# An encoder layer on one core: the mixer's projection units in quarters over all levels, VectorE's unit work one level later, ScalarE's high parts behind its keys, and transposes of the out projection moved up

## What is computed

```python
def hybrid_mixer(u, w_in, attn_sink, attn_out_norm, lb_fwd, lb_bwd, hg_out_norm, w_out, layer):
    proj = u @ w_in                       # (512, 1024) @ (1024, 3328)
    q, k, v, hq, hf_fwd, hf_bwd, hi, hg = jnp.split(proj, cuts, axis=-1)
    q = partial_rope(q...); k = partial_rope(k...)
    att = rmsnorm(windowed_gqa_sink(q, k, v, attn_sink), attn_out_norm)   # 8 heads, window 128
    qh = sigmoid(hq); vh = silu(hi)                                       # 4 heads of 128
    o_fwd = hgrn2_direction(qh, vh, hf_fwd, lbf)      # gated linear recurrence, f = lb + (1-lb)*sigmoid
    o_bwd = flip(hgrn2_direction(flip(qh), flip(vh), flip(hf_bwd), lbb))
    o = rmsnorm(o_fwd + o_bwd, hg_out_norm) * silu(hg)
    return concatenate([att, o]) @ w_out
```

## Time and profile before

| | |
|---|---|
| median of 3 runs | 1089.02 us (1088.95 to 1090.69) |
| the profiled execution, own time | 1084.51 us |
| its span, first to last instruction | 1082.7 us |
| TensorE busy | 1055.2 us, 97% |
| VectorE, ScalarE, GpSimd busy | 39%, 34%, 42% |
| mean granted TensorE clock | 0.990 of full |

### The profile page before, as it was taken

How to read it: one execution, slowest core, us unless ns; L and a number is a source line. 1 busy time by engine, 2 the same in 40 slices (tenths; PEclk the granted TensorE clock), 3 DMA queues, 4 the chain that set the end, 5 groups by cost and what they waited for, 6 DMA issues and landing times.

```text
span 1082.7 us, 13358 instructions
## 1 busy us (share of the span) xinstructions
PE 1055.2 (97%) x5075; PEld 872.4 (81%) x5075; DVE 423.3 (39%) x605; ACT 371.3 (34%) x558; POOL 452.8 (42%) x299
## 2 busy tenths in 40 slices
PE   6999999999999999999998989999999999999997
PEld 5988888888888878888776768788888888888886
DVE  5443434343000351556554565545343434320103
ACT  6322222222122354416665465343222222221211
POOL 3444444444444158842524123035444444444440
PEclk9999999999999999999998989999999999999999
DMA  6333333333433244331111013024333333333312
GB/s 217 97 98 96 98 96 97 97 97 98 136 98 97 59 134 117 78 97 40 39 37 43 1 41 116 20 78 117 92 101 89 103 88 101 91 102 114 97 51 78
DMA packets 136300, 96.00 MB, mean 89 GB/s; under 512 B 11442, under 2 KB 120387, under 8 KB 136260
## 3 DMA queue, kind: packets, MB, share of 16 engines
q1 hardware_dynamic: 136080, 95.43, 29.3%
q10 hardware_dynamic: 180, 0.02, 0.0%
HBM read 93.34 MB, written 2.10 MB: 88 GB/s over the span
## 4 chain that ended last, share of the span: by engine, by line
PE 93%; DVE 3%; ACT 2%; issue 1%; DMA 1%; ACTq 0%; DVEq 0%
PE ps L873 19%; PE ps L874 18%; PE ps L875 18%; PE ps L880 9%; PE ps L881 9%; PE ps L882 9%; PE ps L1039 2%; PE ps L1131 2%; PE ps L1154 2%; PE ps L1073 1%; DVE YB L1326 1%; PE ps L1141 1%; ACT SQX L540 1%; PE ps L898 1%; PE ps L1050 1%
## 5 line engine op out<-in xcount | busy, mean ns | idle before, releaser
L439 POOL TENSOR_TENSOR WL<-raw,WH 128x1024 fp32r<-128x1024 f32 x132 | 317.9, 2410 | 426.2 <-ACT WH L518 426.2
L873 PE MATMUL ps<-XH,WH 128*128 128x512 f32 (+1 forms) x944 | 359.6, 381 | 0.1
L875 PE MATMUL ps<-XH,WL 128*128 128x512 f32 (+1 forms) x944 | 355.0, 376 | 0.0
L874 PE MATMUL ps<-XL,WH 128*128 128x512 f32 (+1 forms) x944 | 354.9, 376 | 0.0
L518 ACT ACTIVATE WH<-raw 128x1024 fp32r<-128x1024 f32 x162 | 171.1, 1057 | 341.5 <-PE ps L875 187.3
L873 PEld LDWEIGHTS ps<-XH,WH 128*128 128x128 f32 x944 | 178.7, 189 | 41.0 <-issue 9.5
L875 PEld LDWEIGHTS ps<-XH,WL 128*128 128x128 f32 x944 | 178.4, 189 | 32.2
L874 PEld LDWEIGHTS ps<-XL,WH 128*128 128x128 f32 x944 | 178.6, 189 | 31.5 <-issue 0.5
L456 POOL TENSOR_TENSOR WL<-raw,WH 128x256 fp32r<-128x256 f32 x120 | 95.1, 825 | 127.8 <-ACT WH L518 127.6
L880 PE MATMUL ps<-WH,hh 128*128 128x512 f32 x352 | 137.1, 390 | 0.0
L882 PE MATMUL ps<-WL,hh 128*128 128x512 f32 x352 | 137.0, 389 | 0.0
(11 more groups left out here) (164 smaller groups left out, 896.7 us busy)
## 6 DMA issues: line engine op xcount, KB each, us to landing
raw<-ffn_w_gate SPq DMA_DIRECT2D x44, 512.0 KB, 3.7
raw<-ffn_w_up SPq DMA_DIRECT2D x44, 512.0 KB, 3.7
raw<-ffn_w_down SPq DMA_DIRECT2D x44, 512.0 KB, 3.7
raw<-w_in SPq DMA_DIRECT2D x22, 512.0 KB, 3.6
raw<-w_out SPq DMA_DIRECT2D x8, 512.0 KB, 3.2
X<-x SPq DMA_DIRECT2D x4, 512.0 KB, 7.0
raw<-w_in SPq DMA_DIRECT2D x8, 256.0 KB, 3.3
out<-X SPq DMA_DIRECT2D x8, 256.0 KB, 2.0
```

The costliest lines, as they stand in the source:

```text
L439: pool.tensor_tensor(low, raw[:, s, :], high.bitcast(fp32), ALU.subtract).then_inc(lo_done, 1)
L873: nc.tensor.matmul(dst, WH[:, s, w], xh, start=first, stop=False)
L874: nc.tensor.matmul(dst, WH[:, s, w], xl, start=False, stop=False)
L875: return nc.tensor.matmul(dst, WL[:, s, w], xh, start=False, stop=last)
```

## The change

**Table.** `mixer_beats` gives each level a count of quarters (2 of the 8 blocks, 6 matmuls): 3 in levels 0 to 9, 2 in level 10, then 1 or 2 in every level to 40, but for 22 (none). Units 7 and 8 now come whole before the loop (before: 7 alone). `values` comes behind a level's parts, a transpose of a `k`, `v` or `q` unit two levels after the unit is done, ahead of the parts.

**VectorE.** `copy_even` and `take_attention` come earlier in a level; the sum of a block's weights is a function of its own, one level earlier; the copy or gate of a unit comes one level after the unit is done, and behind `att_max`. Root, scaling and transposes of the attention and of the recurrence outputs move one level down.

**ScalarE.** `copy_odd` is first in a level, the keys next, and a unit's high part (`ahead`) behind them. `high_o(0)` moves behind the loop.

**Output projection.** `turn_att(2)`, `turn_att(3)` and `turn(2, 0)` go up, the last from behind chunk 2's eight blocks into their middle; with them `high_att(3)`, `low_att(3)`, and `add_y(2, 3)` goes ahead of `split_low(2, 2)`. `turn_o(1)` goes behind the last `values`.

No matmul, elementwise operation or load is added or taken away.

```diff
-    counts = [(2, 1, 2, 1, 2, 1, 2, 1, 2, 1, 1), (0, 1, 1, 1, 1, 1, 1, 1, 0, 0, 0), (0, 1, 1, 1, 1, 1, 1, 1, 0, 0, 0),
-              (0, 1, 1, 1, 1, 1, 1, 0, 0, 0, 0)]
-    halves = [(n, p) for n in range(4 + 3, MIX_UNITS) for p in range(2)]
...
+    counts = (3,) * 10 + (2,) + (1, 1, 1, 1, 1, 2, 1, 1, 1, 1, 1) + (0, 2, 1, 2, 1, 1, 1, 1, 1, 1, 1) + (1, 2, 1, 2, 1, 2, 1, 2, 0, 0, 0)
+    parts = [(n, p) for n in range(4 + 3, MIX_UNITS) for p in range(4)]
+    return parts[:8], [[parts.pop(8) for _ in range(c)] for c in counts]
...
+        MADE = [[n for n, p in parts if p == 3] for parts in BEAT] + [[], []]
...
-        TURN_BEAT, HIGH_BEAT, ROOT_BEAT = 41, 42, 36
+        TURN_BEAT, HIGH_BEAT, ROOT_BEAT = 42, 43, 37
... ScalarE
-                ahead(MIX + min(at + 3, MIX_UNITS + 3))
+                if att_item(i - 2) and i % 2:
+                    copy_odd(i - 2)
                 if g < 7:
                     mix_keys(h, g)
                 elif g >= 8:
                     copy_scores(h, g)
-                if att_item(i - 2) and i % 2:
-                    copy_odd(i - 2)
+                ahead(MIX + min(at + 3, MIX_UNITS + 3))
                 if att_item(i):
                     exp(i)
...
+            high_o(0)
             copy_odd(ITEMS - 1)
...
             high_att(2)
+            high_att(3)
             square_y(2, 0, 0)
             first_y(2, 0)
             first_x(2, 0)
-            high_att(3)
... TensorE
+                for n in MADE[k - 2]:
+                    if n in COPIED:
                         turn_unit(n)
-                    else:
-                        values(n)
+                for n, p in BEAT[k]:
+                    part(n, p)
+                if k and not k % 11:
+                    values(k // 11 - 1)
                 if att_item(i - 1):
                     att_turn(i - 1)
...
             values(NH - 1)
+            turn_o(1)
             att_turn(ITEMS - 1)
...
+            turn_att(2)
             out_tile(0, 6)
             out_tile(0, 7)
-            turn_att(2)
+            turn_att(3)
             for n in range(4, 8):
                 out_tile(1, n)
             for n in range(8):
-                if n == 3:
-                    turn_att(3)
+                if n == 4:
+                    turn(2, 0)
                 out_tile(2, n)
-            turn(2, 0)
... VectorE
+                if att_item(i - 2) and not i % 2:
+                    copy_even(i - 2)
                 if g == 0:
                     diagonal(h)
                 elif g < 8:
...
-                if att_item(i - 2) and not i % 2:
-                    copy_even(i - 2)
+                if att_item(i - 3) and (i - 3) % HQ == HQ - 1:
+                    take_attention((i - 3) // HQ)
+                for n in MADE[k - 2]:
+                    if n in COPIED:
+                        turned(n)
                 if att_item(i):
                     att_max(i)
-                if att_item(i - 3) and (i - 3) % HQ == HQ - 1:
-                    take_attention((i - 3) // HQ)
+                if att_item(i - 2) and (i - 2) % HQ == HQ - 1:
+                    weights_sum((i - 2) // HQ)
+                for n in MADE[k - 1]:
+                    if n in COPIED:
+                        copy_unit(n)
+                    elif n in GATES:
+                        out_gate(n)
...
             take_y(0)
             add_y(2, 0)
-            low_att(3)
             normed(2, 0)
...
             take_y(3)
+            add_y(2, 3)
             split_low(2, 2)
-            add_y(2, 3)
```

More of the change, by code:

```diff
@@ L790, in _ @@
             at = 7
-            for what, n, p in FIRST:
-                if p:
+            for n, p in FIRST:
+                if p == 3:
                     at = n + 1
@@ L813, in _ @@
                     high_att(0)
-                elif k == HIGH_BEAT + 1:
-                    high_o(0)
-                for what, n, *p in BEAT[k]:
-                    if what == "half" and p[0]:
-                        at = n + 1
-                        if MIXU[n][0] == "head":
-                            head_sigmoid(n)
-                        elif MIXU[n][0] == "gate":
-                            out_gate_sigmoid(n)
-                    elif what == "values":
-                        take_values(n)
+                for n in MADE[k]:
+                    at = n + 1
+                    if MIXU[n][0] == "head":
+                        head_sigmoid(n)
+                    elif MIXU[n][0] == "gate":
+                        out_gate_sigmoid(n)
+                if h and not g:
+                    take_values(h - 1)
                 if att_item(i - 4) and (i - 4) % HQ == HQ - 1:
                     square_att((i - 4) // HQ)
+            high_o(0)
             copy_odd(ITEMS - 1)
@@ L1213, in out_tile, with part @@
                     mm.then_inc(y_ready, 1)
-            def half_unit(n, p):
+            def part(n, p):
                 if not p:
                     bank_free(n)
-                half(MIX + n, ps[bank_of(n)], p)
-            for what, n, p in FIRST:
-                half_unit(n, p)
+                quarter_unit(MIX + n, ps[bank_of(n)], p)
+            for n, p in FIRST:
+                part(n, p)
             for k in range(BEATS):
```

79 lines of the change are left out of this document (23 added, 56 removed).

## The result

| | before | after |
|---|---|---|
| median of the runs | 1089.22 us (1088.95 to 1090.69, 4 runs) | **1065.08 us** (1064.66 to 1065.40, 4 runs) |
| profiled execution, span | 1084.51, 1082.7 us | 1065.40, 1063.6 us |
| mean granted clock of it | 0.990 | 0.999 |

The ratio is 0.9775, 95% interval 0.9758 to 0.9792: 24.1 us less, where 19.8 were forecast. From profiled execution to profiled execution the forecast was 1064.7 and 1065.4 came. One run of `spread_hi` (experiment 6) took 2710 us at full clock, from a cause that no run shows, and is left out of its ratio and range; without it the median is 1065.07.

The account below looks back on a forecast made before the run. TensorE, busy 97% of the span, bounds the kernel, so only its waits and low clock can be regained. 7.6 + 6.4 + 1.1 + 4.1 + 1.2 - 0.6 = 19.8 us; 1089.0 - 19.8 = 1069.2 us, range 1065 to 1078.

Parts of the forecast that it names:

- Item 1: Levels 30 to 32: later gate, copy ahead of the tree and a quarter as cover remove waits and low clock; gain 7.6 us.
- Item 2: Levels 38 to 43: 3.5 us of waits and 2.9 us of clock loss go; gain 6.4 us.
- Item 3: Levels 19, 21, 41, 43: four waits for ScalarE's copy go (1.5 us), unit 25's gate costs 0.4; gain 1.1 us.
- under 2 us in all: Sign that the forecast is right: TensorE's waits from L1115 (transposes) and L1128 (values) total less than 2 us.
- Item 4: More runs of unit matmuls, 40 levels against 33, each first matmul slower: 0.6 us lost.
- Item 5: Output projection and first FFN units: chunk 3's wait with its clock goes, 4.1 us, and the last norm's wait, 1.2 us.
- Item 6: Edits put at nothing, such as high parts behind the keys, units 7 and 8 ahead of the loop, later transposes.
- A: Rival: the clock falls all the same, with one or all of 9.0 us kept; 1071 to 1078 us, chance 0.15.
- C: Rival: short levels bound by VectorE throughout, slower in all 28 levels with quarters; 1093 us, chance 0.04.
- D: Rival: output projection's turn waits for the norm, or gates' waits move one level on; 1073 us for the first, chance 0.05.
- B: Rival: small waits in a third to half of 28 levels, 5 to 7 us lost; 1074 to 1076 us, chance 0.10.
- the prediction's rule on the tables: Levels 12 to 21 on ScalarE: a skill's 1.38 us drain per table switch would add 9.7 us; sum uses 1.28 us loads.

Follow-up runs that it names:

- spread_hi: Changed kernel with one quarter moved from level 16 to 15, one from 40 to 41, and the high part behind the exponential: 1065.12 us, ratio 0.9787.
- experiment 6: Two variants of the changed kernel with two quarters moved and the high part behind the exponential, the second also editing level 41's high part: 1065.12 and 1063.85 us.
- experiment 1: Kernel before, unchanged, run again: 1088.51 us, ratio 0.9992; changed kernel, unchanged, run again: 1065.12 us, ratio 0.9794.
- act_only: Kernel before with ScalarE's new order alone: 1084.21 us, ratio 0.9972.
- no_cover: Changed kernel without the quarters of levels 30 to 32, which levels 27 to 29 carry instead: 1066.02 us, ratio 0.9802.
- both_orders: Kernel before with VectorE's and ScalarE's new orders; halves, gates and output projection as they were: 1073.45 us, ratio 0.9869.
- halves_late: Changed kernel with levels 0 to 10 filled with quarters and halves as before from level 12 on: 1068.16 us, ratio 0.9818.
- dve_order: Kernel before with VectorE's new order alone (even copy first, block ahead of the maximum, weights' sum a level earlier): 1082.46 us, ratio 0.9965.
- halves_table: Changed kernel with the table of halves from before, level 0 left empty: 1071.80 us, ratio 0.9859.

## Why the prediction was right or wrong

**The step that failed** is "The median of the runs is 4.5 us above that execution; I carry the difference along, since no row says what makes it". The 4.5 us are, for all but some 0.5, low clock behind the very waits that the change takes away (experiment 1). The sum of the parts, 19.8 us, came out as 19.1 from span to span; without the carried 4.5 the forecast would have been 1064.7. I had allowed 2 us for what it hides; by the ratio, 0.9775 of 1089.0 is 1064.5 us, 0.5 below the low end of the range. A slip in the bounds: items 1 and 3 in full add 0.3 + 0.35, not 1.

**Item 1** (7.6 us): right in size, in part wrong in cause. Levels 30 to 32 take the 13 us forecast, without the wait that I allowed. Of the three edits that it names, the copy ahead of the tree is part of VectorE's new order, without which 2.85 us of wait and the fall stay (`act_only`). With both new orders in place the quarter as cover is worth 0.9 us (`no_cover`) and the later gate 0.1; what these two give without the orders was not run. What item 1 leaves out: with neither of them, the wait falls to 1.0 us and the clock stays once the block also goes ahead of the maximum and GpSimd's low part is no longer beside the tree (`both_orders`). In the changed kernel itself the low part is gone from there (583.33 on), but L459 stands beside the tree's second operation, 1.10 us, and the quarter covers it. I had the tree's 1.2 us in the earlier trace rows and the remark "with operations at 0.7 instead of 1.2 it would be done before", and did not ask what made them 1.2.

**Item 2** (6.4): waits and fall are gone, for the reason given. Here the orders alone are not enough (2.14 us and a fall in `both_orders`), and the later gates do count: made at once, they cost 8.2 us, in levels 41 and 42.

**Item 3** (1.1): the four small waits went, but 2.6 us came in levels 15, 41 and 42 instead of 0.4. So the sign "under 2 us in all" was missed, and the gain was put 2.2 us too high. I named VectorE's gate as what is late; it is ScalarE's high part and table load ahead of the exponential for level 42, and a copy behind a sigmoid in levels 15 and 41.

**Item 4** (0.6 lost): not measured by itself. It is contained in the comparison with `halves_late`, in which the quarters gain 3.0 us in all.

**Item 5** (5.3): 6.6 alone, 6.0 as the last part; right, with 0.4 to 1.3 us more than its waits and its clock account for.

**Item 6** (edits at nothing): "High parts behind the keys" was no edit at nothing. Its readers indeed do not feel it, but the order is worth 4.2 us alone and 6.1 in the changed kernel, by what stood behind the high part on ScalarE and beside the low part on VectorE. The remark on level 0 was right: 3.3 us without its quarters.

**The rivals.** A, C and D did not come: the clock is 1.00 from 430 us on and the levels with one quarter take 4.3 us (587.58 - 583.28) as forecast. Of B, small waits, 2.6 us came in three levels, where it had 5 to 7 in nine or more. On the clock, each fall here stands behind a wait or two, of which the longest is 1.3 to 3.3 us, and it goes when they are closed. The strict reading of the Trainium skill, "TensorE: Matmul & The Clock Gate", section "HAM oscillation — how this bites in real kernels", by which only a longer gap would do it, is not borne out by these runs.

**The two directions differ.** Taking a part out of the changed kernel costs 0.9 (cover), 3.0 (quarters), 6.0 (output projection), 6.1 (ScalarE) and 8.2 us (gates); putting it alone into the kernel before gives 5.8 (VectorE), 4.2 (ScalarE), 6.6 (output projection), and 15.0 for both orders. These are differences of medians. The sums do not match the 24; I take it, without a run that shows it by itself, that a wait closed gives its own length, and the last of the waits that bring the clock down gives the clock too.

## What to carry to other kernels

A profile shows one execution: where its granted clock has stretches below full, look at the clock of every timed run, and count the gap between execution and median among what the waits cost, as it goes with them. Before a wait is put down to missing cover, read the queue of the engine that is waited for: what stands ahead of the awaited instruction, and whether another engine's work beside it makes it longer. Judge a set of such edits together, for one alone may close a wait by half and leave the clock down.

## What the runs showed of the hardware

- **VectorE's tree and GpSimd's low part lengthen each other.** The same operation on 128x512 values takes 0.68 us alone and, in level 30, 1.06 to 1.21 beside L456, whose four parts then take 3.67 us instead of 2.77 (`both_orders` against `dve_order`). The block, of the same size but read from PSUM, keeps its 0.68 beside L456 (`dve_order`, 585.68). It is not always VectorE that pays: in the kernel before the two at 440.01 and 441.21 take 0.69 and 0.70 beside L456, and L456 takes 3.82. GpSimd in the kernel before, level 30, beside the two of 1.20 in the earlier trace rows:

```profile
583.82 3.67 POOL L456 TENSOR_TENSOR WL<-raw,WH 128x256 fp32r<-128x256 f32 x4 [1.20 <-ACT WH L518]
```

The Trainium skill, "SBUF — State Buffer", section "SBUF: two separate sides", states a port pair that VectorE and GpSimd share under an exclusive lock, for VectorE operations with two inputs in SBUF too. The rows agree in that both sides grow and that the operation with an input in PSUM does not; which of them held it in turn is not in them.

- **The clock after the same wait is not the same from run to run.** Level 30 with 3.5 us of waits had 0.79 or 0.50 over the same 20 us; in `halves_late`, the mean clock was 0.999 in two runs and 0.994 to 0.996 in three. Where the longest wait of the mixer was 1.06 us or less, it fell in no profile, though one timed run of `no_cover` (longest wait 1.02 in its profile) had a clock of 0.996. One wait of 1.32 did bring it down (`halves_late`); others of 1.34 (`halves_table`), 1.53 (`spread_hi`) and even 2.45 (`dve_order`, chunk 3 of the output projection) did not. So no length of a wait divides the two cases here.

- **A table load takes 1.28 us and nothing more**: the exponential starts 0.01 us behind it (636.96 + 1.28 = 638.24, and 638.25), and the load 0.02 us behind the high part (635.87 + 1.07 = 636.94). The drain that the prediction's rule on the tables speaks of is on neither side.
